# Order of the high and low matmuls in the wide projection loop of a streaming-encoder layer

## The reference

```
h = rmsnorm(x);  u = h @ w_in                    # 2048 -> q, k, v, forget, xs, B, C, z, dt
x = x + concat(fox_attention(q, k, v, f), ssd_mixer(xs, B, C, z, dt)) @ w_out
h = rmsnorm(x);  g, up = split(h @ w_gate_up)    # 2048 -> 2 x 5632
x = x + (silu(causal_dwconv3(g)) * up) @ w_down  # 5632 -> 2048
x = x + sigmoid(rmsnorm(x) @ w_ple_gate) * (p @ w_ple_proj)
out = rmsnorm(x)
```

## Time and profile before

| | us |
|---|---|
| median of 3 runs (lowest, highest) | 1229.74 (1228.66, 1229.97) |
| the profiled execution | 1229.75 |
| its span | 1228.0 |
| PE busy | 1216.1 |
| DVE busy | 817.7 |
| ACT busy | 642.6 |

### The profile page before, as it was taken

The page is one execution under the profiler, slowest core; times in us unless marked ns, Lnnn a source line. Parts: engine busy times, 40 slices in busy tenths (PEclk is TensorE's granted clock), DMA queues, the critical chain, the costliest instruction groups (busy, mean ns, idle before and its releaser), DMA issues.

```text
span 1228.0 us, 18695 instructions
## 1 busy us (share of the span) xinstructions
PE 1216.1 (99%) x6538; PEld 1042.5 (85%) x6538; DVE 817.7 (67%) x1100; ACT 642.6 (52%) x879; POOL 47.8 (4%) x68
## 2 busy tenths in 40 slices
PE   9999999999999999999999999999999999999997
PEld 8888888888888888888888888888888888888885
DVE  5798787888766667677676776776745454545554
ACT  6455786676555444454444454544434443435555
POOL 2200220002100000000000000000000000000000
PEclk9999999999999999999999999999999999999999
DMA  9566885445655666666666666666655656566652
GB/s 280 172 187 176 243 243 177 126 126 174 201 185 175 189 193 190 190 183 193 195 184 193 188 188 188 188 189 189 194 195 189 191 188 191 187 199 217 195 194 102
DMA packets 184344, 231.66 MB, mean 189 GB/s; under 512 B 11088, under 2 KB 135076, under 8 KB 184164
## 3 DMA queue, kind: packets, MB, share of 16 engines
q1 hardware_dynamic: 182436, 225.92, 60.0%
q0 software_dynamic: 1824, 5.04, 1.4%
q10 hardware_dynamic: 32, 0.01, 0.0%
HBM read 227.22 MB, written 2.14 MB: 187 GB/s over the span
## 4 chain that ended last, share of the span: by engine, by line
PE 97%; DVE 1%; ACT 1%; issue 0%; DMA 0%; ACTq 0%; DVEq 0%
PE ps L380 36%; PE ps L382 18%; PE ps L1031 7%; PE ps L1033 7%; PE ps L1032 6%; PE ps L414 6%; PE ps L415 6%; PE ps L416 6%; PE ps L356 2%; PE ps L823 1%; PE ps L945 0%; PE ps L928 0%; PE ps L907 0%; PE ps L894 0%; ACT w_hi L340 0%; DVE w_lo L345 0%
## 5 line engine op out<-in xcount | busy, mean ns | idle before, releaser
L345 DVE TENSOR_TENSOR w_lo<-w_raw,w_hi 128x1024 fp32r<-128x1024 f32 x412 | 506.4, 1232 | 340.7 <-ACT w_hi L340 339.2
L380 PE MATMUL ps<-h_parts,w_hi 128*128 128x512 f32 x1920 | 670.0, 395 | 0.0
L340 ACT ACTIVATE w_hi<-w_raw 128x1024 fp32r<-128x1024 f32 x412 | 435.4, 1059 | 438.6 <-PE ps L382 249.9
L382 PE MATMUL ps<-h_parts,w_lo 128*128 128x256 f32 x1920 | 533.4, 278 | 0.0
L380 PEld LDWEIGHTS ps<-h_parts,w_hi 128*128 128x128 f32 x1920 | 360.1, 188 | 83.0
L382 PEld LDWEIGHTS ps<-h_parts,w_lo 128*128 128x128 f32 x1920 | 361.0, 188 | 0.1
L1031 PE MATMUL ps<-w_hi,act_parts 128*128 128x512 f32 x352 | 137.2, 390 | 0.0
L1033 PE MATMUL ps<-w_hi,act_parts 128*128 128x512 f32 x352 | 137.0, 389 | 0.0
L1032 PE MATMUL ps<-w_lo,act_parts 128*128 128x512 f32 x352 | 136.9, 389 | 0.0
L1033 PEld LDWEIGHTS ps<-w_hi,act_parts 128*128 128x128 f32 x352 | 66.1, 188 | 13.8
L1031 PEld LDWEIGHTS ps<-w_hi,act_parts 128*128 128x128 f32 x352 | 66.1, 188 | 13.6
(11 more groups left out here) (257 smaller groups left out, 930.8 us busy)
## 6 DMA issues: line engine op xcount, KB each, us to landing
w_raw<-in_w_gate_up SPq DMA_DIRECT2D x352, 256.0 KB, 3.1
w_raw<-in_w_down SPq DMA_DIRECT2D x88, 512.0 KB, 4.5
w_raw<-in_w_in SPq DMA_DIRECT2D x87, 512.0 KB, 4.0
w_raw<-in_w_out SPq DMA_DIRECT2D x32, 512.0 KB, 4.5
w_raw<-in_w_ple_gate SPq DMA_DIRECT2D x32, 512.0 KB, 4.6
ssd_spread<-ssd_rows_dram POOLq DMA_DIRECT2D x16, 192.0 KB, 4.3
w_raw<-in_w_ple_proj SPq DMA_DIRECT2D x4, 512.0 KB, 5.0
out_x<-xtok SPq DMA_DIRECT2D x8, 256.0 KB, 2.9
```

The source lines that it names most:

```text
L340: act.activation(parts(n)[0], w_raw[:, n % RING, :], ACT.Copy).then_inc(w_hi_made, 1)
L345: dve.tensor_tensor(lo, w_raw[:, n % RING, :], hi, ALU.subtract).then_inc(w_lo_made, 1)
L380: pe.matmul(ps[:, bank_of[m], :], hi, both.rearrange("p b t -> p (b t)"), start=first and k == 0, stop=False, skip_group_check=True)
L382: mm = pe.matmul(ps[:, bank_of[m], T:2 * T], lo, both[:, 0, :], start=False, stop=last and k == tiles // len(bank_of) - 1, skip_group_chec ...
```

## The change

The two matmuls of a tile are no longer neighbours. The low one of tile 0 goes first; from then on the low one of tile i + 1 is issued, then the high one of tile i. The last tile's high one ends the chunk and raises w_used. The flag that clears a bank moves to the low matmul of the bank's first tile, the stop flag to the high one of its last.

```diff
--- before.py
+++ after.py
@@ -373,13 +373,18 @@
 
             pe.wait_ge(w_lo_made, n + RING * q + 1)
             tiles = CHUNK // P
+
+            def low(i):
+                k, m = divmod(i, len(bank_of))
+                pe.matmul(ps[:, bank_of[m], T:2 * T], w_lo[:, n % RING, i * P:(i + 1) * P], both_of(k)[:, 0, :],
+                          start=first and k == 0, stop=False, skip_group_check=True)
+
+            low(0)
             for i in range(tiles):
                 k, m = divmod(i, len(bank_of))
-                both = both_of(k)
-                hi, lo = (w[:, n % RING, i * P:(i + 1) * P] for w in (w_hi, w_lo))
-                pe.matmul(ps[:, bank_of[m], :], hi, both.rearrange("p b t -> p (b t)"),
-                          start=first and k == 0, stop=False, skip_group_check=True)
-                mm = pe.matmul(ps[:, bank_of[m], T:2 * T], lo, both[:, 0, :],
+                if i + 1 < tiles:
+                    low(i + 1)
+                mm = pe.matmul(ps[:, bank_of[m], :], w_hi[:, n % RING, i * P:(i + 1) * P], both_of(k).rearrange("p b t -> p (b t)"),
                                start=False, stop=last and k == tiles // len(bank_of) - 1, skip_group_check=True)
             return mm.then_inc(w_used, 1)
```

## The result

| | before | after |
|---|---|---|
| median, us | 1229.55 (1228.66 to 1230.61, 6 runs) | 1233.87 (1233.27 to 1234.97, 6 runs) |
| ratio after to before | | 1.0034, 95% interval 1.0024 to 1.0044 |
| span of the profiled execution, us | 1228.0 | 1231.9 |

The account below looks back on a forecast made before the run. TensorE's matmul pace was taken as the bound, busy 1216.1 of 1228.0 us. From 1229.75 us, gate/up 0 and projection 0 to -2.0 us gave 1229.5 us, no change; the eight-in-ten range was 1219.5 to 1238.5 us.

Parts of the forecast that it names:

- Which pace the stream falls into: Mixed matmul stream: irregular steps may redraw the pace, 346.6 or 353.5 ns a pair; the term that could not be fixed.
- the term of gate/up: Gate/up stage, 1408 high-low matmul pairs: the change was summed as 0 us there.
- no change: Whole kernel: likeliest case, 1229.5 us, its own range 1227.7 to 1232 us, chance 0.38.
- the second rival: Gate/up chunks take the long pace after the reordering: +6.0 to +9.4 us, 1235.8 to 1239.1 us, chance 0.35.
- its sentence on every other chunk: Gate/up: if only every other chunk takes the long pace, about half the loss, 1233 us.
- Its price per long chunk: Gate/up: a chunk at the long pace costs 34 to 48 ns more.
- 346.6 = 226.7 + 120: Gate/up pair at the short pace equals plain 512-column plus plain 256-column matmul, in ns, leaving nothing for bank conflicts.
- the plain prices: Start-to-start times in streams of one size: 226.7 ns per 512-column matmul, 120 ns per 256-column one.
- the 10 ns on the release: Chunk end: w_used, moved to a high matmul, is released 10 ns later; cost 0 because ScalarE and evacuation have slack.
- the projection's sum: Projection's 64 wide chunks, 37 long and 27 short: change between 0 and -2.0 us, taken a little towards 0.
- the banks, 0: Matmul writes to PSUM: a same-bank step was taken to cost nothing, with an upper bound of 6.6 ns a pair.
- The rival "faster": Same-bank steps cost something in the mixed stream; avoiding them in gate/up gives 1220.4 us, at half 1225.1; chance 0.27.

Follow-up runs that it names:

- The grouped kernel: Against the kernel before, each chunk issues all eight low matmuls, then all eight high ones; 1233.27 us, ratio 1.0027.
- Both bank kernels: Changed order with neighbours sharing a bank as before the change: 1233.72 us; old order with every gate/up neighbour on another bank: 1230.01 us.
- the strictly alternating one: Against the kernel before, low matmul one tile ahead, the first tile's low one near the chunk's end, no double steps; 1229.38 us, ratio 1.0001.

## Why the prediction was wrong

The failing step is **"Which pace the stream falls into"**, and the choice built on it: the term of gate/up stood in the sum with 0 and measured +4.0 us (489.52 to 493.55). I had found both paces and written that irregular steps may shift the stream between them, then made "no change" the likeliest case at 0.38. The runs put the second rival in its place: its sentence on every other chunk gave 1233 us, and 1233.87 was measured by just that, a long chunk after each short one. Its price per long chunk was right, 34 to 48 ns foreseen, 47 measured. Its mechanism was not: it had every entry from a plain stream come out at the long pace and gave no reason for every other chunk, so that this figure came so close is partly luck.

What misled me stands one part earlier. **346.6 = 226.7 + 120** looked like a proof that the short pace has no surcharge and is the natural state. The grouped kernel shows that the plain prices don't add up: with the two sizes nearly unmixed a chunk is 2.80 us and not 2.77. The double steps themselves took together what was foreseen, 346 to 348 ns a chunk against 346.7, though neither the 120 ns nor the 227 that were to confirm the plain prices was found (113 to 116 and 232 to 233); what they do to the pairs around them is what counts.

Right were: no instruction, wait or release costs anything (no idle time ahead of the matmul lines, the 10 ns on the release hidden by ScalarE's waiting); the projection's sum, 0 within the 2 us allowed (0.14 us less ahead of gate/up), since its long chunks and its short ones only change places (by the starts 37 of 64 are long before and after, and 28 have changed their pace); and **the banks, 0**. Both bank kernels show it; the Trainium skill's page "PSUM — Partial Sum Buffer", section on bank collisions, names no cost for two full-array matmuls that follow each other on one bank, and they agree. The rival "faster" at 0.27 had no more behind it than that the mixed stream had not been tested.

Open remains what holds a stream at one pace for 450 us and lets a small step move it to the other. Two paces were seen where the low matmul's columns take about as long as a weight load or less (192 and 256 columns), one where they take longer (320), and with a narrow stationary for the low matmul the changed order's two chunk lengths fell and its loss was gone. That points to the load, but no run changes the load alone, and how load and column stream would hinder each other in a cycle of three pairs is not shown.

No kernel here that keeps all products beats the one before; the strictly alternating one equals it.

## What to carry to other kernels

Where a short matmul took about as long as the load of the next stationary (here 256 columns against 128 columns of weights), the pace of the stream depended on the order of sizes, by up to 2% a pair; with 320 columns it still did, by 0.4% a chunk and the other way. Keep one strict alternation and count matmuls per stretch in the trace before and after any reordering. Don't spread accumulation over banks for TensorE's own sake: here a step within a bank cost no more than one to another. And a price that equals the sum of two plain streams is no proof that mixing them is free: run them apart in the same loop to see.

## What was not expected of the hardware

- Two stable paces of the same instruction stream at full clock, 346.6 and 353.5 ns a pair, each kept over several chunks or many without any wait in the trace; the long one is a cycle of three pairs, 361, 349 and 350 ns.
- Taking a quarter of the columns from every second matmul (192 for 256) saved 2.2 ns of 346.6 a pair; adding a quarter (320) cost 33.
- An edit in order alone was worth +4.3 us at 256 columns and -2.5 us at 320.
